# Expert down-projection loads issued on the scalar engine's queue, gate and up loads alone on the sync engine's queue

## What is computed

```python
_, gsel = lax.top_k(lg, 1)                       # 1 of 4 groups
top_v, top_i = lax.top_k(le_sel, TOP_K_IN_GROUP) # 2 of its 8 experts
expert_id = gsel * EXPERTS_PER_GROUP + top_i
act = silu(einsum("td,edf->tef", hf, w_gate)) * einsum("td,edf->tef", hf, w_up)
out = einsum("tef,efd->td", act * combine[..., None], w_down)
```

## Time and profile before

| | us |
|---|---|
| median of 3 runs | 1108.48 |
| lowest and highest | 1103.89, 1109.3 |
| profiled execution, its own time | 1104.57 |
| its span | 1102.8 |
| TensorE busy | 1064.1 (96%) |
| VectorE, ScalarE, GpSimd busy | 695.9, 289.4, 186.2 |
| DMA moved | 204.97 MB, 186 GB/s over the span |

### The profile page before, as it was taken

One profiled execution on the slowest core, in us unless ns is written; L12 is line 12 of the kernel. 1 busy time (PEld: TensorE's weight loads), 2 busy tenths in 40 slices (PEclk: granted clock), 3 DMA queues, 4 the chain that ended last, 5 costly groups with the idle time before them and its releaser, 6 DMA issues.

```text
span 1102.8 us, 15605 instructions
## 1 busy us (share of the span) xinstructions
PE 1064.1 (96%) x6135; PEld 607.6 (55%) x6135; DVE 695.9 (63%) x1385; ACT 289.4 (26%) x588; POOL 186.2 (17%) x229
## 2 busy tenths in 40 slices
PE   6999999999999999999999999989999999998996
PEld 4666766787764445888766645545533333333331
DVE  5576699947858665743376676877754455555453
ACT  5200341567821111100033301111411222222223
POOL 4000200101000000000000000000123445554455
PEclk9999999999999999999999999999999999999999
DMA  9109450297546004100244450015889999999962
GB/s 297 56 1 213 46 43 1 92 276 257 216 170 182 1 1 155 74 1 1 85 183 154 155 226 39 20 58 208 299 283 412 413 413 413 414 415 412 413 256 82
DMA packets 75468, 204.97 MB, mean 186 GB/s; under 512 B 25592, under 2 KB 34448, under 8 KB 67056
## 3 DMA queue, kind: packets, MB, share of 16 engines
q1 hardware_dynamic: 54336, 168.82, 43.4%
q0 software_dynamic: 20928, 35.09, 9.6%
q10 hardware_dynamic: 128, 0.03, 0.0%
HBM read 195.23 MB, written 52.18 MB: 224 GB/s over the span
## 4 chain that ended last, share of the span: by engine, by line
PE 77%; DMA 10%; DVE 5%; ACT 2%; SPq 2%; issue 2%; ACTq 0%; POOL 0%; POOLq 0%; DVEq 0%
PE bank L832 16%; PE bank L1004 9%; PE bank L1069 9%; PE bank L1304 8%; DMA arena<-in_w_up 7%; PE bank L1199 6%; PE bank L1318 4%; PE bank L802 3%; PE bank L963 3%; PE bank L1101 3%; PE bank L1166 3%; DMA arena<-in_w_down 2%; DMA arena<-work_rows,slots_in 1%; SPq L487 1%; PE bank L1248 1%
## 5 line engine op out<-in xcount | busy, mean ns | idle before, releaser
L832 PE MATMUL bank<-arena 128*128 128x360 f32 (+1 forms) x576 | 177.7, 468 | 0.9 <-DVE arena L1881 0.9
L1304 PE MATMUL bank<-arena 128*32 128x512 f32 x1536 | 172.3, 599 | 5.9 <-DMA arena<-in_w_up 5.9
L832 PEld LDWEIGHTS bank<-arena 128*128 128x128 f32 x576 | 108.5, 190 | 64.7 <-issue 1.4
L1304 PEld LDWEIGHTS bank<-arena 128*32 128x32 f32 x1536 | 50.4, 110 | 107.5 <-issue 107.1
L2200 DVE TENSOR_TENSOR arena<-arena,bank 128x512 f32<-128x512 f32 (+3 forms) x56 | 68.4, 1221 | 64.9 <-PE bank L1069 37.4
L1004 PE MATMUL bank<-arena 128*128 128x272 f32 x448 | 103.0, 392 | 0.0
L1199 PE MATMUL bank<-arena 128*128 128x512 f32 x224 | 100.6, 598 | 2.2 <-DVE arena L2365 2.2
L1069 PE MATMUL bank<-arena 128*128 128x512 f32 x224 | 97.7, 593 | 0.0
L1004 PEld LDWEIGHTS bank<-arena 128*128 128x128 f32 x448 | 85.0, 190 | 17.4
L1318 PE MATMUL bank<-arena 128*32 128x512 f32 x768 | 87.5, 593 | 1.3 <-DMA arena<-in_w_down 0.8
L2696 DVE SCALAR_TENSOR_TENSOR arena<-arena 128x1024 f32<-128x1024 f32 x22 | 45.8, 2083 | 66.5 <-ACT arena L1763 66.5
(11 more groups left out here) (474 smaller groups left out, 1457.3 us busy)
## 6 DMA issues: line engine op xcount, KB each, us to landing
arena<-in_w_gate SPq DMA_DIRECT2D x32, 1024.0 KB, 18.9
arena<-in_w_up SPq DMA_DIRECT2D x32, 1024.0 KB, 25.1
arena<-in_w_down SPq DMA_DIRECT2D x32, 1024.0 KB, 26.4
arena<-in_ck SPq DMA_DIRECT2D x8, 1024.0 KB, 7.1
arena<-in_cv SPq DMA_DIRECT2D x8, 1024.0 KB, 5.4
arena<-in_w_in SPq DMA_DIRECT2D x3, 2048.0 KB, 13.7
work_firsts<-in_x SPq DMA_DIRECT2D x1, 4352.0 KB
arena<-in_x SPq DMA_DIRECT2D x8, 512.0 KB, 5.9
```

What stands on the lines that cost most here:

```text
L832: last = nc.tensor.matmul(b[:, 0:w], win[slot][:, k, m * P:m * P + P], ht[:, k, c0:c0 + w], start=k == 0, stop=k == KD - 1)
L1304: last = nc.tensor.matmul(bank[2 + j % 2][t0:t0 + QT, :].rearrange("p (h n) -> p h n", h=2), (xgt[j % 2] if j else xgt_first)[:, k, t0:t0 ...
```

## The change

The 27 down loads of the loop leave the sync engine. ScalarE issues each of them on its own queue, right behind main_copy(j) of the expert's last round, for j from 1 to 20, into the same slots and with the same semaphores. The sync engine's loop keeps gate and up loads alone and no longer waits for d_full. The first five down loads stay where they are.

```diff
-            for j in range(NR + 1):
+            for j in range(NR):
                 for e in range(NE - GUB):
                     if last_round(e) == j:
                         sp.wait_ge(sem["gu_full"], j + 1)
                         load_gu(e + GUB, e % GUB, sem[f"gu_in{e % GUB}"])
-                for e in range(NE - DNB):
-                    if last_round(e) == j - 1:
-                        sp.wait_ge(sem["d_full"], j)
-                        load_dn(e + DNB, e % DNB, sem[f"dn_in{e % DNB}"])
...
                 if j < NR - 2:
                     main_copy(j)
+                    for e in range(NE - DNB):
+                        if last_round(e) == j:
+                            act.dma_start(dn[e % DNB][:, :, :], I["w_down"][EXPERT[e + DNB]].rearrange("(k p) n -> p k n", p=P)).then_inc(sem[f"dn_in{e % DNB}"], 16)
                 if j == NR - 2:
```

## The result

| | before | after |
|---|---|---|
| median, us | 1107.0 (4 runs) | 1129.88 (4 runs, 1127.01 to 1132.64) |
| ratio, 95% interval | | 1.0213 (1.0192 to 1.0234) |
| profiled span, us | 1102.8 | 1128.4 |

The change makes the kernel slower, by 2.1% (the interval reaches from 1.9% to 2.3%). The forecast was slower too, by 0.7%; the measured time lies inside the whole range (1101 to 1133) but above that of the forecast's own case (1109 to 1127), and the loss is nearly three times what was taken.

What follows compares the result with a forecast made beforehand. Bound: DMA bandwidth, 12.6 us of work per round against TensorE's 11.67. 1104.57 + 4 (traffic coming forward) + 4 (idle DMA engines) = 1112.6 us, 1116.5 on the median's footing; range 1101 to 1133.

Steps and rivals of the forecast that it cites:

- the forecast's own case: Expert stage: gathered rows late by turns, 1116.5 us on the median's footing, range 1109 to 1127, chance 0.46.
- the one for one turns: DMA engines in the expert stage: full q0 and q1 alternate packet for packet, 10666 against 10365, despite q1's longer packets.
- the three way turn of 0.53 us: DMA engine with three full queues: one packet of each per cycle, 0.316 + 0.158 + 0.057 us; today 0.29 us.
- weights that run ahead: Expert rounds: gate and up weights gain 23.5 packets per round and engine, at most five slots ahead, for 3.4 rounds.
- the gathered rows as the place where it bites: Head of a round: TensorE transposes rows fetched through q0; no slack there, so any longer latency stops TensorE.
- steps (2) to (4): Down-load issue on ScalarE, hidden by 7 us; loads about 1.3 us later, taken as 0; sync engine freed, no gain by itself.
- step (5): DMA engines: three full queues give weights 89% not 81%; GpSimd's 44.8 packets take 23.8 us per round, then 20.1.
- Term (b): Expert stage: DMA engines idle while weights lack a free slot and GpSimd awaits a landing; 0 to 11.5 us, taken 4.
- R4: Expert stage: slower by more, 1134 us through lower granted clock after waits, or ScalarE stuck in a full queue; chance 0.08.
- Term (a): Kernel's tail: weights ahead leave no traffic for after the last wait, so it comes forward; 0 to 5.5 us, taken 4.
- The sign that the prediction gave for it: Kernel's tail: little of q1 or q10 moved after the last wait.
- R2: Whole kernel: no change, since full engines move the same bytes; 1108.5 us, chance 0.30.

Runs made afterwards that it cites:

- run 1: Kernel before, sync engine issuing each down load only after ScalarE has copied the down product out, same queue: 1107.15 us, ratio 1.0001.
- run 2: Changed kernel with the loop's gate and up loads also issued by ScalarE, on the down loads' queue, so two busy queues again: 1106.7 us, ratio 0.9991.
- run 3: Kernel before with down weights laid out for 8 KB packets, half as many, same bytes and queue: 1123.95 us, ratio 1.0185.
- run 4: Changed kernel with each gate and up load split in two, so that all weight packets are 4 KB: 1116.09 us, ratio 1.0109.
- run 8: Changed kernel with GpSimd issuing the gather of input rows ahead of the store and the gather of first results: 1127.24 us, ratio 1.0195.
- run 10: Changed kernel with the input-row gather first on GpSimd, and VectorE's product and row weights ahead of its sum: 1122.49 us, ratio 1.0163.

## Why the prediction was right in direction and wrong in size

**Right.** The bound of the kernel before (full engines, 12.6 us of DMA work per round), the one for one turns, the three way turn of 0.53 us (0.50 measured), weights that run ahead, the gathered rows as the place where it bites, ScalarE's issue at 0.4 us and hidden (0.374 in the median), q10's 28 MB. Runs 1 and 2 show that steps (2) to (4) cost nothing, as taken, and runs 3 and 4 that step (5), the turn, is what costs. Two readings were off without bearing on the forecast: today's mean packet of q1 is 0.814 x 178 x 16 / 10666 = 0.217 us by the earlier trace rows and not 0.237, and the 8047 small packets are not all masked rows, since they hold packets that belong to the transfers themselves too (each down load shows 272 packets on q10, 16 more than its 256 pieces of 4 KB).

**Term (b) was mis-sized.** It took 4 us for idle DMA engines with a cap of 11.5. From the first gate and up product to 46.8 us ahead of the end (781.9 to 1056 before, 785.3 to 1081.6 after) the stage grew by 22.2 us, and the engines moved 109.46 MB in it where before moved 107.76; 1.70 MB are 4.1 us at 413 GB/s. By this estimate the other 18 us are engines without work, over four times what was taken and over the cap. Two pieces can be pointed at: in 866 to 1044 the kernel after moved 69.22 MB where before moved 73.57, and 4.35 MB are 10.5 us; 1060 to 1070 adds (413 - 197)/413 x 10 = 5.2 us. The line is 866 to 1044 of the kernel after.

```profile
DMA packets 19163, 69.22 MB, mean 389 GB/s; under 512 B 7029, under 2 KB 7029, under 8 KB 14430
```

The sentence that failed is "Once weights are ahead, their queues run dry within a round, q0 catches up in those gaps". It took q0 as a pile of packets that waits to be served. It is a chain: the product's rows are stored, the store lands, the first results are gathered, they land, VectorE adds them, and behind that sum in VectorE's order stand the next product and the next row, on whose signal the next store and the next gather go out. While three queues are full, each link takes longer: ahead of its gathers of first results GpSimd waited 16.9 us in nine pieces for a store to land before, and 36.6 in nine after, both from 780 us on (lines below). When the weight slots are full, the engines are free, but the chain has too little queued to use them: 152 GB/s in 980 to 990. Then freed slots fill the queues again and it repeats. The rows above show two such turns, at 970 and at 1050.

```profile
POOL arena L655 <- DMA work_firsts<-arena,slots_in: 16.9, 9, 3.7
POOL arena L651 <- DMA work_firsts<-arena,slots_in: 36.6, 9, 7.9
```

The prediction named VectorE nowhere in that chain. It looked for the first place where a later landing meets TensorE (the row gathers, with no slack) and stopped there; run 8 shows that a second place with about the same price lay right behind it (22.2 us of waits for VectorE's product in place of 22.8 for rows).

**The clock was left out of the sum.** It stood in a rival of its own (R4) at a chance of 0.08. The waits did bring it in: granted clock 0.77 and 0.89 in 970 to 990, 0.70 in 1050 to 1060, and some 6.8 us in the stage. It belonged to the forecast as a share of the longer waits: the earlier trace rows showed 1.7 us behind a wait of 2.0. Not every wait brings it. Behind the row waits of 2.33, 3.43, 6.32 and 5.32 us the gate and up product took 8.62, 7.66, 8.66 and 8.76 us; behind those of 1.15, 1.78 and 2.45 us it took 7.07 or 7.08.

**Term (a)** (4 us, traffic coming forward) was about right. In the last 46.8 us before moved 6.16 MB and after 4.50; 1.66 MB at 413 GB/s are 4.0 us, and 1.41 MB of them are weights (2.46 MB on q1 before, 1.05 on q10 after). The sign that the prediction gave for it does not show, though: after its last row wait at 1055 the kernel after still moved 2.80 MB on q1 and 3.38 on q10, because that wait lies further ahead of the end.

**A sign of being wrong came true.** The prediction said that it is wrong if the gathers' latency stays as it is. In the median it did not rise in 876 to 1020 (15.2 us; before 15.9), only its spread (4.4 to 24.2; before 12.4 to 17.4), because fast and slow stretches alternate. What stops TensorE are the slow ones: the rows issued at 952.44 ended the wait of 6.32 us at 976.72. And R2, by which full engines and the same bytes give the same time, did not hold: bytes were the same, and the engines did not stay full.

What stays open is how the 22 us of the stage divide between the row gathers and the chain by VectorE. With the row waits taken away (run 8) the time stayed where it was, with VectorE's order changed as well (run 10) 7 of the 23 us went; VectorE's order changed alone was not run.

## What to carry to other kernels

Moving transfers to a second queue does not only add issue capacity, it changes who gets the DMA engines: each busy queue gets a packet per cycle, whatever its size and urgency. Before opening a queue (or lengthening packets), count the packets that the queue with the latency-bound chain needs in front of its waited-for transfer, and price each at the sum of one packet of every other busy queue. And when a loop has a chain of landings (store, gather, sum), follow it once round, over all the engines that keep it in order, before saying that full engines regulate it.

## What the runs showed of the hardware

Packets of 8 KB, of 4 KB and of under 512 B count as one turn each: 317, 323 and 321 packets on three queues in 10 us. With two queues, longer packets on one of them slowed the kernel by 1.85%, with no other change than the column order of a transpose, and TensorE waited for gathered rows (18.3 us); shorter ones slowed it by 0.5%, and it waited for weights (12.1 us). That fits a turn ratio that sets which kind of data comes late. One issue of a down load held ScalarE for 6.08 us where it issues all weights (run 2), and the sync engine for up to 6.05 us; with a queue of their own, down loads took ScalarE 0.37 us in the median.
